# Gated delta-rule heads on one core: the projection fillers of the chunk scan as 256-column halves, five per chunk instead of two whole ones

## What is computed

```python
qkv = silu(causal_dwconv(h @ in_w[:, :o1], conv_w))   # per head: q, k, v; z from the same product
g = cumsum of log-decays inside a chunk; beta = sigmoid(...)
a_mat  = strict_lower((k*beta) @ k.T * decay)          # per chunk
t_mat  = inverse(a_mat + I)
w, u   = t_mat @ (k*beta*exp(g)), t_mat @ (v*beta)
attn   = lower((q @ k.T) * decay)
for each chunk:                                        # the scan, state S
    v_new = u - w @ S
    o     = (q*exp(g)) @ S + attn @ v_new
    S     = S * e_last + k_dec.T @ v_new
o = rmsnorm(o) * silu(z);  out = o @ out_w
```

## Time and profile before

| | |
|---|---|
| median of 3 runs | 2101.68 us (2100.63 to 2105.51) |
| profiled execution: its own time | 2100.75 us |
| its span | 2098.8 us |
| PE, share of the span busy | 98% |
| DVE, ACT, POOL | 64%, 30%, 12% |
| granted TensorE clock, mean | 0.997 |

### The profile page before, as it was taken

One profiled execution on the slowest core, in us unless ns is written; L12 is line 12 of the kernel. 1 busy time (PEld: TensorE's weight loads), 2 busy tenths in 40 slices (PEclk: granted clock), 3 DMA queues, 4 the chain that ended last, 5 costly groups with the idle time before them and its releaser, 6 DMA issues. The chain is left out here.

```text
span 2098.8 us, 20772 instructions
## 1 busy us (share of the span) xinstructions
PE 2047.3 (98%) x6914; PEld 1044.5 (50%) x6914; DVE 1351.1 (64%) x1900; ACT 630.7 (30%) x1051; POOL 244.7 (12%) x188
## 2 busy tenths in 40 slices
PE   7999999999999999999998999999999999999998
PEld 4444444446566566656454454544444444444443
DVE  3787753266756656666823697439999997434633
ACT  4345531223443443443213410013211112241021
POOL 0000001113213213211102100011000000003200
PEclk9999999999999999999999999999999999999999
DMA  9333389241111211111420316389522222333021
GB/s 349 124 116 112 97 282 237 84 101 38 48 31 36 47 31 36 47 32 35 148 36 20 131 51 113 91 233 250 127 58 78 66 71 65 110 105 130 20 100 60
DMA packets 243824, 207.17 MB, mean 99 GB/s; under 512 B 52204, under 2 KB 202785, under 8 KB 243745
## 3 DMA queue, kind: packets, MB, share of 16 engines
q1 hardware_dynamic: 213393, 157.25, 25.1%
q0 software_dynamic: 13056, 42.99, 8.3%
q10 hardware_dynamic: 17312, 6.10, 1.3%
HBM read 182.55 MB, written 60.33 MB: 116 GB/s over the span
## 5 line engine op out<-in xcount | busy, mean ns | idle before, releaser
L2345 PE MATMUL bank<-hT,ring 128*128 128x512 f32 x576 | 254.2, 592 | 0.0
L2345 PE MATMUL bank<-resid,ring 128*128 128x512 f32 x432 | 191.3, 592 | 0.0
L2345 PEld LDWEIGHTS bank<-hT,ring 128*128 128x128 f32 x576 | 109.4, 190 | 137.8 <-issue 136.6
L1312 PE MATMUL bank<-hT,ring 128*128 128x512 f32 x336 | 157.7, 595 | 1.8 <-ACT silu_z L1549 1.8
L3265 DVE SCALAR_TENSOR_TENSOR yT<-s_arena,yT 128x1024 f32<-128x1024 f32 x120 | 152.8, 1273 | 0.0
L3265 DVE SCALAR_TENSOR_TENSOR s_arena<-s_arena 128x1024 f32<-128x1024 f32 x112 | 142.6, 1273 | 0.0
L2317 PE MATMUL bank<-hT,ring 128*128 128x512 f32 x320 | 139.4, 594 | 0.0
L2345 PEld LDWEIGHTS bank<-resid,ring 128*128 128x128 f32 x432 | 82.1, 190 | 103.3 <-issue 102.6
L2317 PEld LDWEIGHTS bank<-hT,ring 128*128 128x128 f32 x320 | 60.1, 190 | 73.7 <-issue 73.5
L2390 PE MATMUL bank<-ssm_y,ring 128*128 128x512 f32 x192 | 83.4, 592 | 0.0
L1312 PEld LDWEIGHTS bank<-hT,ring 128*128 128x128 f32 x336 | 58.4, 190 | 49.9 <-issue 49.5
(11 more groups left out here) (585 smaller groups left out, 3595.1 us busy)
## 6 DMA issues: line engine op xcount, KB each, us to landing
ada<-in_ada_w SPq DMA_DIRECT2D x8, 2048.0 KB, 8.1
ring<-in_gdn_in_w SPq DMA_DIRECT2D x32, 512.0 KB, 4.1
ring<-in_w_in SPq DMA_DIRECT2D x54, 256.0 KB, 2.9
ab_U_sums<-in_w_in POOLq DMA_DIRECT2D x6, 2048.0 KB, 19.2
resid<-in_x SPq DMA_DIRECT2D x8, 1024.0 KB, 8.8
ring<-in_lru_in_w SPq DMA_DIRECT2D x16, 512.0 KB, 3.9
ring<-ab_U_sums SPq DMA_DIRECT2D x32, 256.0 KB, 2.9
lru_arena<-in_ada_w SPq DMA_DIRECT2D x6, 1024.0 KB, 13.7
```

Of the source, the lines that this page charges most:

```text
L1312: last = nc.tensor.matmul(bank[:, to, :], w[:, k, :], v[:, k, :], start=(first and k == 0), stop=(k == KB - 1), skip_group_check=not only)
L2345: last = nc.tensor.matmul(bank[:, to, :], w[:, k, :], src[:, k, :], start=(start and k == 0), stop=(k == HK - 1), skip_group_check=not alone)
```

## The change

In the last six products of `project_pairs` each matmul of 512 columns becomes two of 256 (`parts=2`), so that `fill` takes halves there. In the scan a chunk now takes two halves behind `read`, two behind `new` (each pair is what one whole filler was), and one more half ahead of the `read` of chunks 1 to 7 (in the last head one whole matmul of the output projection there). Ahead of `k_flip` stand two whole fillers fewer, ahead of `q_flip` one fewer, and behind the scan seven halves are left instead of four whole fillers. Counted in whole fillers, the scan has 20.5 instead of 17 of the 56. On ACT the copies C21a, `kept1b` and `kept2b` move one chunk later.

```diff
--- before.py
+++ after.py
@@ -1306,14 +1306,16 @@
-                        def product(pr, to, w, v, name, first=False, only=False):
-                            w = blocks(pr)[w]
+                        def product(pr, to, w, v, name, first=False, only=False, parts=1):
+                            w, width = blocks(pr)[w], HALF // parts
                             for k in range(KB):
-                                last = nc.tensor.matmul(bank[:, to, :], w[:, k, :], v[:, k, :], start=(first and k == 0), stop=(k == KB - 1),
-                                                        skip_group_check=not only)
-                                if k == KB - 1:
-                                    px_pe.mark(last, name + pr)
-                                yield
+                                for n in range(parts):
+                                    cols_ = slice(n * width, (n + 1) * width)
+                                    last = nc.tensor.matmul(bank[:, to, cols_], w[:, k, :], v[:, k, cols_], start=(first and k == 0 and n == 0),
+                                                            stop=(k == KB - 1), skip_group_check=not only)
+                                    if (k, n) == (KB - 1, parts - 1):
+                                        px_pe.mark(last, name + pr)
+                                    yield
@@ -1344,19 +1346,19 @@
-                        yield from product("a", 0, "A22", tok_sum4, "P4")
+                        yield from product("a", 0, "A22", tok_sum4, "P4", parts=2)
...
-                        yield from product("b", 2, "S4", tok22, "P3")
+                        yield from product("b", 2, "S4", tok22, "P3", parts=2)
...
@@ -1412,7 +1414,7 @@
-                        fill(4, 0)
+                        fill(2, 0)
...
-                        fill(13, 18)
+                        fill(12, 18)
@@ -1471,17 +1473,18 @@
                         for c in range(NCH):
                             if c == 0:
-                                fill(1, 0)
+                                fill(2, 0)
...
                             else:
+                                fill(1, 1)
                                 hd_dve.wait(pe, f"mem{c - 1}", h)
...
-                            fill(1, 2)
+                            fill(2, 2)
                             hd_dve.wait(pe, f"delta{c}", h)
...
-                            fill(1, 2)
+                            fill(2, 2)
                             hd_act.wait(pe, f"new{c}", h)
@@ -1622,13 +1625,13 @@
-                            if c == 1 and after is not None:
+                            if c == 2 and after is not None:
                                 px_pe.wait(act, "P4a", h)
...
-                            if c == 2 and after is not None:
+                            if c == 3 and after is not None:
                                 keep(1, "b", h, "P6", "C12")
-                            if c == 4 and after is not None:
+                            if c == 5 and after is not None:
                                 keep(2, "b", h, "P5", "C22")
```

More of the change, by code:

```diff
@@ L1346, in project_pairs @@
                         tok_sums.wait(pe, "T4")
-                        yield from product("a", 0, "A22", tok_sum4, "P4")
+                        yield from product("a", 0, "A22", tok_sum4, "P4", parts=2)
                         sums["b"].wait(pe, "S2", h)
                         px_act.wait(pe, "kept0b", h)
-                        yield from product("b", 3, "S2", tok_sum2, "P6")
+                        yield from product("b", 3, "S2", tok_sum2, "P6", parts=2)
                         px_dve.wait(pe, "C12a", h)
-                        yield from product("b", 2, "S1", tok_sum1, "P5", first=True)
+                        yield from product("b", 2, "S1", tok_sum1, "P5", first=True, parts=2)
                         px_act.wait(pe, "kept1b", h)
-                        yield from product("b", 3, "S3", tok_sum3, "P7")
+                        yield from product("b", 3, "S3", tok_sum3, "P7", parts=2)
                         sums["b"].wait(pe, "S4", h)
                         px_act.wait(pe, "kept2b", h)
-                        yield from product("b", 2, "S4", tok22, "P3")
+                        yield from product("b", 2, "S4", tok22, "P3", parts=2)
                         px_dve.wait(pe, "C22b", h)
-                        yield from product("b", 3, "A22", tok_sum4, "P4")
+                        yield from product("b", 3, "A22", tok_sum4, "P4", parts=2)
                     def partial_out():
```

## The result

| | before | with the change |
|---|---|---|
| median, with its runs | 2100.63 us (9) | 2109.27 us (9) |
| lowest to highest | 2098.46 to 2105.51 | 2105.06 to 2113.32 |
| profiled execution, its span | 2100.75, 2098.8 us | 2110.32, 2108.4 us |
| mean granted TensorE clock | 0.997 | 0.993 |
| a middle head, read 0 to read 0, mean of six | 78.01 us | 78.15 us |

The ratio is 1.0035, interval 1.0025 to 1.0045: slower by a third of a per cent, more than the 0.2% that the prediction took for the least that can be told from no change. A second set of 11 runs gave 1.0032 (1.0021 to 1.0042).

The account below looks back on a forecast made before the run. Between scan and next head an ACT, DVE, POOL and DMA chain was taken to end together with PE's work. From 2100.75 us, 8.6 (scan) - 6.0 + 0.0 + 0.2 = +2.8 gave 2103.6 us, range 2097.5 to 2109.5.

Parts of the forecast that it names:

- The chunk: In the scan: period 3.26 us instead of 3.18, +0.08 seven times, so +0.6 us a head.
- A half costs half: Split filler matmuls: at most 0.005 us extra a record, at most 0.2 us a head, left to the range.
- The stall at P3b: Behind `read` of chunk 6 PE waits for ACT's copy `kept2b`: 0.63 us a head.
- From E to the F flip: From the scan's end (E) to the next head's flip F: F comes 1.0 us earlier, -6.0 in six heads.
- The middle heads: From state read to state read: heads of about 78.2 us instead of 78.0.
- The first head: Way to its inversion: no gain, as its POOL mask waits behind weight sums that nothing moves; 0.
- The last head: Seven chunks of 5.41 us instead of 4.81, +4.2; flip behind the scan earlier, -3.7; with earlier `y`, +0.2.
- 1: Rival: PE is the bound everywhere and the chain moves with it; -10.6, 2090.2 us; chance 0.10.
- 2: Rival: behind the scan the decays start no earlier, only `y`'s 0.3 comes off; +7.0, 2107.8 us; chance 0.22.
- 3: Rival: in the scan no stall at P3b, the copy comes in time; -1.6, 2099.2 us; chance 0.15.
- 4: Rival: the halves' doubled weight loads show, 4.8 us a head, 34 in all; 2135 us; chance 0.03.
- the upper side: Whole run: slower than before by over 0.2%, given 0.32; within 0.56, faster 0.12.

Follow-up runs that it names:

- e4: The change with ACT's decays ahead of its copy of P1a and DVE's C12b moved to chunk 7; 2098.77 us, 0.9984 of before.
- e7: Before, scan untouched, with the decays ahead of the copy of P1a and C12b in chunk 7; 2101.17 us, 0.9998 of before.
- e1: The change without output matmuls ahead of the last head's state reads, so eight lie behind its scan again; 2106.21 us, 1.0020 of before.
- e11: The change with eight useless matmuls added in PE's wait for `o_tok` ahead of the last outputs' flip; 2103.96 us, 1.0012 of before.
- e6: Before with the fillers of five products in halves, two halves for each whole in every chunk, no place moved; 2102.22 us, 1.0001 of before.
- e10: Before with only the last head's part: one output matmul ahead of each state read but the first; 2104.83 us, 1.0015 of before.
- e3: Before with five products' fillers in halves, but chunks 0 and 1 left at one half where a whole stood; 2115.36 us, 1.0072 of before.
- e5: The change with the edits of e1 and e4 and ACT's three copies back at chunks 1, 2 and 4; 2091.23 us, 0.9957 of before.
- e8: As e5, with three output matmuls moved to ahead of the last head's first state read; 2092.04 us, 0.9959 of before.

## Why the prediction came out as it did

- **The chunk** (+0.08): 0.10 in the chunk shown. **A half costs half**: 0.004 a record measured, within the bound of 0.005. These 0.15 us a head were left to the range.
- **The stall at P3b** (0.63): 0.52. The copy starts 1.20 behind its `mem`, to the hundredth as foretold, but PE goes on at its end with the load alone; the 0.10 for an uncovered load was not needed. Undoing it gave back 0.62 a head.
- **From E to the F flip** (-1.0): the decays came 1.16 earlier, F 1.24 (E+40.31 against E+41.55); PE's two waits are 0.30 and 0.58, where 0.3 and 1 were said. The chain bounds it, as said; e4 and e7 show it from both sides.
- **The middle heads** were to be 0.2 longer and are 0.14 longer. **The first head**: it waits 2.73 us for `base` in the change, and its first level then runs partly at half clock (3.09 us for the 16 products that take 1.95 elsewhere). Its way from P1a to the first `read` is 0.45 us longer, where 0 was said.
- **The last head** is the step that failed: "seven times +4.2", "-3.7", "+0.2". Each length came true (chunks of 5.41, flip at 3.18 behind the scan), and e1 still gives back about 3 us. The step counted PE time up to the flip. It moved seven of the eight matmuls that covered `o_tok` ahead of the `read`s, as if PE's idle time at two places were worth the same. It isn't: behind the new wait of 2.16 us the clock fell to 1.2 GHz, and e11 shows that this is the price and not a later flip. The prediction did not price the clock at all, though the waits of the middle heads and of the last flip were forecast and one row of before already stood at PEclk 0.95 in this stretch. What e1 does not give back holds, beside the stall, the half clock at the last head's start (1.7 us in the profile) and the stage near 1290 us, and no run shows that the change made these two.
- **The rivals**: 1 would have needed PE to bound everything; heads near 75.5 did not come. 2 gave 2107.8 us, the nearest figure of all, and is wrong: the decays did start earlier (E+10.48, not 11.4). Who had read only the time would have taken it for confirmed. 3 is out, the stall is there. 4 is out by e6: no doubled load shows. The Trainium skill (TensorE: Matmul & The Clock Gate, "Back-to-back issue gap") had given +72 us by my linear reading; the trace's ratio was the right guide.
- **The range** held by luck: 2109.27 is 0.2 us inside 2097.5 to 2109.5. Its upper end stood for rival 2 and a longer stall; neither came, and the clock had no place in it.
- **What was under-weighted** is the upper side: a forecast of +2.8 with an unpriced clock should have put more than 0.32 on slower.

Open: why the wait at the last head's start is followed by half clock in some programs and not in others (before and e10 are the same program up to there). With a wait of 2.14 or 2.15 us seven profiles show half clock behind it and three (before, e3, e6) full pace; the four with 1.55 (e4, e5, e7, e8) all show full pace. No run here changes that alone. The Trainium skill (TensorE: Matmul & The Clock Gate, Part 1: The HAM clock gate) says that the activity which sets the clock is looked at on a schedule of the chip's own that doesn't start with the kernel, so that the point of the change shifts from run to run. The pair of before and e10 agrees with that, 5.39 against 7.06 us behind the same wait, but does not show it; the two profiles of the change, with half clock at the same places, show no such shift. Open too: whether the longer wait near 1290 us has to do with the change.

## What to carry to other kernels

Fillers that cover a gap inside a loop are taken from somewhere: look at what they covered there, in the last iteration above all, where nothing follows to take their place. If an engine gets work off its path, the next chain must be shortened in the same step, or the gain stays locked in as new waits; the two edits here are worth nothing, or a loss, alone, and 0.43% together with the repairs. Price a new wait of TensorE by what the matmuls behind it take, not by its length.

## What the runs showed of the chip that was not expected

Useless matmuls in a wait made the kernel faster: 2 us of them ahead of the last flip took 3.0 us off the 16 records behind it (10.11 to 7.11) and, by ratios, 4.2 us off the run. And a wait of the same length in the same place (2.1 us) was followed by full pace in one program and by 1.7 us more in another, so one profile is not enough to price it.
